# Fetching an expert's three weight matrices as three transfers instead of six halves, in a single-core encoder layer with a mixture of experts

## The chip, the cores and the metric

One core of one Trainium2 chip runs the whole kernel. The metric is the device time of one execution in microseconds (us); lower is better. All arithmetic inputs are float32.

## The reference, cut to what matters

The layer works on 1536 tokens (512 and 1024) with a model width of 1024. After a retention and an attention part it ends in a hierarchical mixture of 32 gated experts, of which each token uses two:

```python
pg = softmax(xt @ w_rg); g_sel = argmax(pg)                     # one of 4 groups
le_sel = (xt @ w_re)[group g_sel]; top_p, top_i = top_k(softmax(le_sel), 2)
gate = p_sel * top_p / sum(top_p)
# the 3072 (token, expert) pairs are sorted by expert and padded to blocks of 128 rows
def expert_block(xb, e):
    return (silu(xb @ w_g[e]) * (xb @ w_u[e])) @ w_d[e]         # 1024->512, 1024->512, 512->1024
y[token] += gate * expert_block(...)                            # two experts add to each token
x = rmsnorm(x + y) * g_final
```

Each expert has a gate, an up and a down matrix of 2 MB, so a block of 128 rows needs 6 MB of weights.

## The kernel before, in words

`build` (line 2010) runs five phases one after the other: `phase_project`, `phase_retention`, `phase_latent`, `phase_mix` (output projection, router, and a table in DRAM that lists for every expert the rows that chose it), and `phase_experts` (line 1671). The change touches the last two.

**Buffers.** `raw` (line 2032) holds one expert's three matrices as they come from DRAM: 128 partitions by 3 matrices by 4096 float32. On a partition a matrix is one run of 16 KB, in DRAM as well (line 2034). There is one `raw`, not two. Each matrix is treated as two halves of 2048 columns; `raw_span` (line 1666) gives the columns of half j, and j runs from 0 to 5: gate 0 and 1, up 2 and 3, down 4 and 5. `w_hi` and `w_lo` (line 1687) hold the same weights split into a rounded part and a rest; a product is made of three matmul passes over them (`three_passes`, line 108).

**Order of a block.** `each_block` (line 1726) runs two blocks written out and then a loop over pairs, 32 blocks in this execution. For block n:

- SyncE, `load` (line 1740): for each half j it waits until VectorE has split that half for block n-1 (`s_wlo[j]`) and then issues the half's transfer of 1 MB (lines 1745 to 1747). The first block's six halves are issued at the end of `phase_mix` (line 1401), before the experts begin.
- ScalarE, `step` (line 1888): `split(j, n)` for j 0 to 3 waits for the half to land (`s_raw[j]`, line 1870) and for the matmuls of the block before that used it, and writes `w_hi`. Then it takes its half of the previous block's result (`take_y`), the silu, `split` 4 and 5, the rounded part of the transposed hidden rows, and `rows_hi(n + 1)`.
- VectorE, `step` (line 1942): after each `w_hi` half it writes `w_lo` (line 1923). The order is halves 0 to 3, `take_y` of the previous block (line 1936), half 4, the product of the silu with the up result (line 1953), the rest of the hidden rows (line 1955), half 5, `rows_lo(n + 1)`.
- TensorE, `step` (line 1828): gate and up matmuls (`e_pg`, `e_pu`), then it waits for the gathered rows of block n+1 (`s_xg`, line 1841) and transposes the first half of them (`e_px`, line 1821), transposes the hidden rows (`e_ph`, line 1846), transposes the other half, and does the down matmuls (`e_py`).
- GpSimd, `step` (line 1786), with a DMA queue of its own: it copies the row numbers and shares of block n, then calls `gather(n + 2, ...)` (line 1766): a load of 128 table rows of 8 bytes (`e_who`, line 1768), a wait for it, an indirect load of 128 activation rows of 4 KB (`e_xg`, line 1772) and one of 128 shares of 4 bytes (`e_part`, line 1775). Then it waits for both halves of the result of block n and issues an indirect store that adds 128 rows of 4 KB into `x_mid` (line 1808).

All transfers, SyncE's (queue q1) and GpSimd's (queue q0), run on the same 16 DMA engines. The lines that set the order of the weight loads are these:

```python
for j in range(6):
    sp.wait_ge(s_wlo[j], n)
    sp.dma_start(raw[:, j // 2, span(j)], w_exp[j // 2][e][:, span(j)]).then_inc(s_raw[j], 16)
```

Of the kernel before, what the change touches and what calls it, by code (L numbers as in the profile page):

```python
# [1305 lines left out]
def phase_mix(nc, mixT, x_all, w_out, w_fold, g_ffn, w_rg, w_re, ident_d, route_d, blocks_d, x_mid, h_rows, table,  # L1306
              gates, blocks, n_pairs, s_tick, s_tock, raw, s_raw0, w_exp, shares):
    with ExitStack() as ctx:
# [60 lines left out]
        @block.sync  # L1369
        def _(sp):  # L1370
            sp.dma_start(ident[:], ident_d).then_inc(s_const, 16)
            sp.dma_start(route[:], route_d).then_inc(s_const, 16)
            sp.dma_start(g_row[:], g_ffn.partition_broadcast(P)).then_inc(s_const, 16)
            sp.dma_start(w_r[:, :, 0:NG], w_rg.rearrange("(p k) e -> p k e", k=KD)).then_inc(s_const, 16)
            sp.dma_start(w_r[:, :, NG:], w_re.rearrange("(p k) e -> p k e", k=KD)).then_inc(s_const, 16)
            sp.dma_start(blocks[:].rearrange("p a n -> p (a n)"), blocks_d).then_inc(s_const, 16)
            sp.dma_start(mx[:, 0, :], mixT[0]).then_inc(s_in[0], 16)
            sp.dma_start(xr[:, 0, :], x_all[0]).then_inc(s_xr[0], 16)
            w_v = w_out.rearrange("(k p) n -> p k n", p=P)
            for k in range(KD):  # L1380
                if k >= 3:
                    sp.wait_ge(s_wlo, k - 2)
                sp.dma_start(stage[:, k % 3, :],
                             w_v[:, k, :] if k < KD // 2 else w_fold[k - KD // 2]).then_inc(s_raw[k % 3], 16)

            def tile(r, half, last):
                t = 2 * r + half
                if not last:
                    behind = not (isinstance(r, int) and r == 0 and half == 0)
                    if behind:  # L1390
                        sp.wait_ge(s_mlo, t)
                        sp.wait_ge(s_const, 96)
                    sp.dma_start(mx[:, 1 - half, :], mixT[t + 1]).then_inc(s_in[1 - half], 16)
                    if behind:
                        sp.wait_ge(s_x2, t)
                        sp.wait_ge(s_const, 96)
                    sp.dma_start(xr[:, 1 - half, :], x_all[t + 1]).then_inc(s_xr[1 - half], 16)

            pairs(sp, TILES, tile)

            for j in range(6):
                sp.dma_start(raw[:, j // 2, raw_span(j)], w_exp[j // 2][0][:, raw_span(j)]).then_inc(s_raw0[j], 16)

        @block.gpsimd
        def _(pool):
# [265 lines left out]
def phase_experts(nc, w_exp, ident_d, h_rows, table, shares, blocks, n_pairs, s_tick, raw, s_raw, x_mid, g_final,  # L1671
# [4 lines left out]
    with ExitStack() as ctx:  # L1676
# [57 lines left out]
        @block.sync  # L1734
        def _(sp):
            sp.dma_start(ident[:], ident_d).then_inc(s_const, 16)
            sp.dma_start(g_row[:], g_final.partition_broadcast(P)).then_inc(s_const, 16)

            def load(r, half):
                n = 2 * r + half  # L1740
                if isinstance(r, int) and n == 0:
                    return
                e = n if isinstance(r, int) else sp.value_load(blocks[0:1, 0, bass.ds(n, 1)], min_val=0,
                                                               max_val=NE - 1)
                for j in range(6):
                    sp.wait_ge(s_wlo[j], n)
                    sp.dma_start(raw[:, j // 2, span(j)], w_exp[j // 2][e][:, span(j)]).then_inc(s_raw[j], 16)

            each_block(sp, load)

            pairs_done = pair_count(sp)
            for half in range(2):
                sp.wait_ge(s_store[half], 16 * pairs_done)
            for j in range(6):
                sp.dma_start(raw[:, j // 2, span(j)].rearrange("p (t n) -> p t n", t=2),
                             x_mid[2 * j:2 * j + 2].rearrange("t p n -> p t n")).then_inc(s_xmid[j], 16)
            for t in range(TILES):
                sp.wait_ge(s_out, t + 1)
                sp.dma_start(out[t], x_sum[t]).then_inc(s_kept, 16)
            sp.wait_ge(s_kept, 16 * TILES)  # L1760
# [106 lines left out]
        @block.scalar  # L1867
        def _(act):
            def split(j, n):
                act.wait_ge(s_raw[j], 16 * (n + 1))  # L1870
                free_after(act, j, n)
                nc.scalar.copy(w_hi[:, j // 2, span(j)], raw[:, j // 2, span(j)]).then_inc(s_whi[j], 1)  # L1872

            def rows_hi(n):
                for b in range(2):
                    act.wait_ge(s_xt, 2 * n + b + 1)
                    nc.scalar.copy(xT_hi[:, b * 512:(b + 1) * 512], px[:, b * 512:(b + 1) * 512]).then_inc(s_xhi, 1)

            def take_y(n, half):

                act.wait_ge(s_y, n + 1)
                act.wait_ge(s_code, n + 3)
                nc.scalar.activation(y_sb[half][:, 0:512], py[:, 0:512], ACT.Copy,
                                     scale=gate[half][:, 0:1]).then_inc(s_ya, 1)

            rows_hi(0)

            def step(r, half):
                n = 2 * r + half
                split(0, n)  # L1890
                split(1, n)
                split(2, n)
                split(3, n)
                if not (isinstance(r, int) and n == 0):
                    take_y(n - 1, 1 - half)
                act.wait_ge(s_gate, n + 1)
                nc.scalar.activation(act_g[:], pg[:], ACT.Silu).then_inc(s_silu, 1)
                split(4, n)
                split(5, n)
                act.wait_ge(s_ht, n + 1)  # L1900
                nc.scalar.copy(hT_hi[:], ph[:]).then_inc(s_hhi, 1)  # L1901
                rows_hi(n + 1)

            each_block(act, step)
            last = act.value_load(n_pairs[0:1, 1:2], min_val=0, max_val=(NE + MORE + 1) // 2)
            take_y(2 * last + 1, 1)

            act.wait_ge(s_eps, 1)

            for t in range(TILES):  # L1910
                act.wait_ge(s_xmid[t // 2], 16)
                act.wait_ge(s_rstd, t)
                one = slice(t, t + 1)
                nc.scalar.activation(junk, x_sum[t], ACT.Square, accum_out=ssq[:, one]).then_inc(s_sq, 1)  # L1914
                act.wait_ge(s_sq, t + 1)
                nc.scalar.activation(root[:, one], ssq[:, one], ACT.Sqrt, bias=eps[:],
                                     scale=1.0 / D).then_inc(s_root, 1)
# [92 lines left out]
def build(nc, d, out):  # L2010

    def scratch(name, shape, dt=F32):
        return nc.dram_tensor("s_" + name, shape, dt, kind="Internal").ap()

    mid = scratch("mid", (TILES, P, M_W))
    mixT = scratch("mixT", (TILES, P, D))
    w_fold = scratch("w_fold", (HM, P, D))
    x_mid = scratch("x_mid", (TILES + 1, P, D))
    h_rows = scratch("h_rows", (ROWS, D))
    shares = scratch("shares", (2 * ROWS, 1))  # L2020
    table = scratch("table", (NE * ROWS, 2), I32)

    with ExitStack() as ctx:
        s_tick, s_tock = (ctx.enter_context(nc.semaphore(n)) for n in ("tick", "tock"))
        phase_project(nc, d["x"], d["w_in"], d["g_mix"], d["g_q"], d["g_kv"], d["rope"], d["ident"], mid)
        phase_retention(nc, mid, d["log_decay"], d["gn_g"], d["dist"], d["index"], d["ident"], mixT)
        phase_latent(nc, mid, d["w_cat"], d["w_out"], d["rope"], d["ident"], mixT, w_fold)
        gates = ctx.enter_context(nc.sbuf_tensor("gates", [P, TILES, 2], F32))
        blocks = ctx.enter_context(nc.sbuf_tensor("blocks", [1, 2, NBLK], I32))
        n_pairs = ctx.enter_context(nc.sbuf_tensor("n_pairs", [1, 2], I32))  # L2030

        raw = ctx.enter_context(nc.sbuf_tensor("raw", [P, 3, 4096], F32))
        s_raw = [ctx.enter_context(nc.semaphore(f"raw{j}")) for j in range(6)]
        w_exp = [d[n].rearrange("e (p k) n -> e p (k n)", p=P) for n in ("w_gate", "w_up", "w_down")]
        phase_mix(nc, mixT, d["x"], d["w_out"], w_fold, d["g_ffn"], d["w_rg"], d["w_re"], d["ident"], d["route"],
                  d["blocks"], x_mid, h_rows.rearrange("(t p) n -> t p n", p=P), table, gates, blocks, n_pairs,
                  s_tick, s_tock, raw, s_raw, w_exp, shares)
        phase_experts(nc, w_exp, d["ident"], h_rows, table, shares, blocks, n_pairs, s_tick, raw, s_raw, x_mid,
                      d["g_final"], out)
# [20 lines left out]
```

## Time and profile before

| What | Value |
|---|---|
| Runs | 1805.31, 1809.92, 1807.42 us; median 1807.42 |
| The profiled execution's own time | 1802.13 us |
| Its span (first to last instruction) | 1800.6 us |
| TensorE matmul busy | 1494.7 us (83%) |
| VectorE busy | 1078.9 us (60%) |
| ScalarE busy | 835.3 us (46%) |
| GpSimd busy | 358.4 us (20%) |
| Read from DRAM / written | 288.61 MB / 63.87 MB |
| Loads into `raw` of gate, up, down | 64 each of 1024 KB; median from issue to landing 6.6, 9.6, 8.2 us |

The expert phase lasts from about 1094 us to the end. Times in rows are microseconds from the start of the span. A line of the timeline has start, duration, engine, source line, operation, output and inputs, and in brackets the idle time before it with what ended it; "x4" means four instructions merged, of which the first start and the whole duration are given.

### The profile page before, as it was taken

The page shows a single profiled execution, that of the slowest core. Times are in us where ns is not written, and L with a number is a line of the kernel's source. Part 1 is how long each engine was busy: PE and PEld are TensorE (multiplying, and loading weights), DVE is VectorE, ACT ScalarE, POOL GpSimd, SP SyncE. Part 2 cuts the span into 40 slices and gives each one's busy share as a digit, 9 for nine tenths or more (in the row PEclk, how much of TensorE's full clock was granted, in tenths as well). Part 3 has the DMA queues.
Part 4 walks back from the last instruction along what each step waited for, and adds up shares of the span by engine and source line. Part 5 has one row for each costly group of instructions (what it writes and reads, how often), then busy time and mean ns, then how long its engine had stood idle before and what let it go on. Part 6 is the DMA issues. An engine that isn't in the chain of part 4 may idle for free. (4 is left out here: it accounts for less than half of the span.)

```text
span 1800.6 us, 21880 instructions
## 1 busy us (share of the span) xinstructions
PE 1494.7 (83%) x7330; PEld 1224.4 (68%) x7330; DVE 1078.9 (60%) x1689; ACT 835.3 (46%) x1139; POOL 358.4 (20%) x327
## 2 busy tenths in 40 slices
PE   6799999954674779996699963999999999999990
PEld 5688888843673657885488852777777777777770
DVE  5322323224774656764345544888788887888784
ACT  5323232321564455543322213776667666766664
POOL 0000000000462000000011213233433433343330
PEclk9899999976675889999699976999999999999995
DMA  7121221224353110001633454999999999999977
GB/s 260 49 97 61 83 83 61 84 81 151 106 175 119 59 65 24 13 12 38 216 116 133 135 215 138 319 359 362 355 355 360 357 361 353 357 361 358 360 234 291
DMA packets 83585, 347.35 MB, mean 193 GB/s; under 512 B 14514, under 2 KB 25922, under 8 KB 57282
## 3 DMA queue, kind: packets, MB, share of 16 engines
q1 hardware_dynamic: 66434, 300.37, 45.6%
q0 software_dynamic: 17104, 46.38, 9.2%
q8 instruction: 26, 0.43, 0.1%
q14 instruction: 21, 0.17, 0.0%
HBM read 288.61 MB, written 63.87 MB: 196 GB/s over the span
## 5 line engine op out<-in xcount | busy, mean ns | idle before, releaser
L1923 DVE TENSOR_TENSOR e_w_lo<-raw,e_w_hi 128x2048 fp32r<-128x2048 f32 x192 | 430.8, 2285 | 40.9 <-ACT e_w_hi L1872 40.9
L1872 ACT CAST e_w_hi<-raw 128x2048 fp32r<-128x2048 f32 x192 | 353.8, 1921 | 0.0
L110 PE MATMUL a_pG<-a_w_hi,a_xT_hi 128*128 128x512 f32 (+1 forms) x480 | 189.8, 395 | 8.7 <-DVE a_w_lo L353 6.1
L112 PE MATMUL a_pG<-a_w_hi,a_xT_lo 128*128 128x512 f32 (+1 forms) x480 | 186.5, 388 | 0.0
L111 PE MATMUL a_pG<-a_w_lo,a_xT_hi 128*128 128x512 f32 (+1 forms) x480 | 186.1, 388 | 0.0
L1772 POOL DMA_INDIRECT e_xg<-s_h_rows,e_who x34 | 84.2, 2477 | 261.3 <-DMA e_who<-s_table 137.9
L110 PE MATMUL e_py<-e_w_hi,e_hT_hi 128*128 128x512 f32 x256 | 104.3, 408 | 30.4 <-DVE e_hT_lo L1955 30.4
L110 PEld LDWEIGHTS a_pG<-a_w_hi,a_xT_hi 128*128 128x128 f32 x480 | 91.2, 190 | 25.9 <-issue 5.5
L110 PE MATMUL e_pg<-e_w_hi,e_xT_hi 128*128 128x512 f32 x256 | 104.3, 408 | 4.9 <-DVE e_w_lo L1923 4.9
L110 PE MATMUL d_po<-d_w_hi,d_mT_hi 128*128 128x512 f32 x192 | 81.7, 426 | 26.0 <-DVE d_w_lo L1552 26.0
L112 PEld LDWEIGHTS a_pG<-a_w_hi,a_xT_lo 128*128 128x128 f32 x480 | 91.1, 190 | 17.2
L111 PEld LDWEIGHTS a_pG<-a_w_lo,a_xT_hi 128*128 128x128 f32 x480 | 91.3, 190 | 15.7
L111 PE MATMUL e_pg<-e_w_lo,e_xT_hi 128*128 128x512 f32 x256 | 101.8, 398 | 0.0
L112 PE MATMUL e_pg<-e_w_hi,e_xT_lo 128*128 128x512 f32 x256 | 101.7, 397 | 0.0
L112 PE MATMUL e_py<-e_w_hi,e_hT_lo 128*128 128x512 f32 x256 | 101.1, 395 | 0.0
L112 PE MATMUL e_pu<-e_w_hi,e_xT_lo 128*128 128x512 f32 x256 | 101.0, 395 | 0.0
L110 PE MATMUL e_pu<-e_w_hi,e_xT_hi 128*128 128x512 f32 x256 | 101.0, 395 | 0.0
L111 PE MATMUL e_pu<-e_w_lo,e_xT_hi 128*128 128x512 f32 x256 | 101.0, 394 | 0.0
L111 PE MATMUL e_py<-e_w_lo,e_hT_hi 128*128 128x512 f32 x256 | 101.0, 394 | 0.0
L1280 DVE TENSOR_TENSOR c_pT_lo<-c_pt,c_pT_hi 128x512 fp32r<-128x512 f32 x80 | 52.1, 684 | 46.8 <-ACT c_pT_hi L1131 46.8
L112 PE MATMUL d_po<-d_w_hi,d_mT_lo 128*128 128x512 f32 x192 | 79.9, 416 | 0.0
L111 PE MATMUL d_po<-d_w_lo,d_mT_hi 128*128 128x512 f32 x192 | 79.9, 416 | 0.0
(314 smaller groups left out, 3092.2 us busy)
## 6 DMA issues: line engine op xcount, KB each, us to landing
raw<-in_w_gate SPq DMA_DIRECT2D x64, 1024.0 KB, 6.6
raw<-in_w_up SPq DMA_DIRECT2D x64, 1024.0 KB, 9.6
raw<-in_w_down SPq DMA_DIRECT2D x64, 1024.0 KB, 8.2
s_mid<-a_rec SPq DMA_DIRECT2D x12, 1536.0 KB
a_x_sb<-in_x SPq DMA_DIRECT2D x12, 512.0 KB, 6.4
b_kv<-s_mid SPq DMA_DIRECT2D x12, 512.0 KB, 4.1
b_qk<-s_mid SPq DMA_DIRECT2D x12, 512.0 KB, 4.1
b_vg<-s_mid SPq DMA_DIRECT2D x12, 512.0 KB, 5.5
```

The lines of the kernel that those rows point to most:

```text
L110: pe.matmul(out, st_hi, mv_hi, start=first, stop=False)
L111: pe.matmul(out, st_hi, mv_lo, start=False, stop=False)
L112: return pe.matmul(out, st_lo, mv_hi, start=False, stop=last)
L1280: nc.vector.tensor_tensor(pT3_lo[:, 4 * i:4 * i + 4, j * P:(j + 1) * P], pt[:, c * 512:(c + 1) * 512].rearrange("p (k i) -> p k i", k=4), ...
L1772: pool.indirect_dma_start(out=xg[half][:], out_offset=None, in_=h_rows, in_offset=bass.IndirectOffsetOnAxis(ap=who[half][:, 0:1], axis=0), ...
L1872: nc.scalar.copy(w_hi[:, j // 2, span(j)], raw[:, j // 2, span(j)]).then_inc(s_whi[j], 1)
L1923: nc.vector.tensor_tensor(w_lo[:, j // 2, span(j)], raw[:, j // 2, span(j)], w_hi[:, j // 2, span(j)].bitcast(F32), ALU.subtract).then_inc ...
```

## The change

The loads of `raw` go from two per matrix to one per matrix, in both places where they are issued. The single load waits for both halves of the matrix to have been split. The semaphores of landing go from six to three, and ScalarE's split of either half waits for the whole matrix. The splits themselves stay in halves, and the order of instructions on ScalarE, VectorE, TensorE and GpSimd stays as it is.

```diff
-            for j in range(6):
-                sp.dma_start(raw[:, j // 2, raw_span(j)], w_exp[j // 2][0][:, raw_span(j)]).then_inc(s_raw0[j], 16)
+            for m in range(3):
+                sp.dma_start(raw[:, m, :], w_exp[m][0]).then_inc(s_raw0[m], 16)
...
-                for j in range(6):
-                    sp.wait_ge(s_wlo[j], n)
-                    sp.dma_start(raw[:, j // 2, span(j)], w_exp[j // 2][e][:, span(j)]).then_inc(s_raw[j], 16)
+                for m in range(3):
+                    sp.wait_ge(s_wlo[2 * m], n)
+                    sp.wait_ge(s_wlo[2 * m + 1], n)
+                    sp.dma_start(raw[:, m, :], w_exp[m][e]).then_inc(s_raw[m], 16)
...
             def split(j, n):
-                act.wait_ge(s_raw[j], 16 * (n + 1))
+                act.wait_ge(s_raw[j // 2], 16 * (n + 1))
...
-        s_raw = [ctx.enter_context(nc.semaphore(f"raw{j}")) for j in range(6)]
+        s_raw = [ctx.enter_context(nc.semaphore(f"raw{j}")) for j in range(3)]
```

## Rows read from the trace of the kernel before

**Rows 1.** Windows, one stretch: us, busy by engine, PE clock, DMA share, GB/s.

```profile
1400.00:1500.00 100.00, 94.50 (x419) 74.23 (x418) 82.25 (x56) 67.84 (x55) 36.97 (x31) 1.00 1.01 359
```

**Rows 2.** Waits, 1200 to 1700 us: who waited for whom, us, times, longest.

```profile
DVE e_w_lo L1923 <- ACT e_w_hi L1872: 28.9, 25, 1.2
...
PEld e_px L1821 <- DMA e_part<-s_shares,e_who: 16.8, 22, 1.3
...
PE e_px L1821 <- DMA e_part<-s_shares,e_who: 6.9, 15, 0.8
```

**Rows 3.** Chain that ended last, one round of two blocks: start, us, what.

```profile
1446.80 0.71 PE e_px L1821 x4
...
1466.83 7.88 DMA e_who<-s_table
...
1475.69 2.69 POOL e_xg L1772
...
1478.69 8.19 DMA e_part<-s_shares,e_who
1486.92 0.71 PE e_px L1821 x4
```

**Rows 4.** Timeline of GpSimd, the adding store of one block.

```profile
1463.39 1.63 POOL L1808 DMA_INDIRECT s_x_mid<-e_y_sb,e_code  x1 [2.91 <-issue]
```

**Rows 5.** Timeline of TensorE, transposes of hidden rows in four blocks.

```profile
1124.81 0.75 PE L1846 MATMUL e_ph<-e_ident,e_h_sb 128*128 128x128 f32 x4 [0.41 <-DVE e_h_sb L1953]
1749.27 0.75 PE L1846 MATMUL e_ph<-e_ident,e_h_sb 128*128 128x128 f32 x4 [0.41 <-DVE e_h_sb L1953]
...
1205.70 0.64 PE L1846 MATMUL e_ph<-e_ident,e_h_sb 128*128 128x128 f32 x4
1225.67 0.75 PE L1846 MATMUL e_ph<-e_ident,e_h_sb 128*128 128x128 f32 x4 [0.41 <-DVE e_h_sb L1953]
```

**Rows 6.** Timeline of SyncE's queue: the two issues of each matrix.

```profile
1459.63 2.54 SPq L1747 DMA_DIRECT2D raw<-in_w_up  x2
1465.93 6.29 SPq L1747 DMA_DIRECT2D raw<-in_w_down  x2
1475.43 2.54 SPq L1747 DMA_DIRECT2D raw<-in_w_gate  x2
```

**Rows 7.** DMA issues: up half issued at 1461.83, down half at 1471.89; us to landing.

```profile
raw<-in_w_up SPq DMA_DIRECT2D x1, 1024.0 KB, 11.1
...
raw<-in_w_down SPq DMA_DIRECT2D x1, 1024.0 KB, 6.4
```

**Rows 8.** Timeline of ScalarE: splits 0 to 3, then splits 4 and 5.

```profile
1469.79 7.36 ACT L1872 CAST e_w_hi<-raw 128x2048 fp32r<-128x2048 f32 x4
...
1481.75 3.70 ACT L1872 CAST e_w_hi<-raw 128x2048 fp32r<-128x2048 f32 x2
```

**Rows 9.** DMA issues: down half issued at 1123.13 onto a nearly empty queue.

```profile
raw<-in_w_down SPq DMA_DIRECT2D x1, 1024.0 KB, 5.9
```

**Rows 10.** DMA queues, 1460 to 1480.1 us (one block): packets, MB, share.

```profile
q1 hardware_dynamic: 866, 6.29, 82.0%
q0 software_dynamic: 352, 0.93, 19.2%
```

**Rows 11.** DMA queues, 1046.5 to 1049.5 us, weights with little beside them.

```profile
q1 hardware_dynamic: 173, 1.21, 96.4%
```

**Rows 12.** DMA queues, 380 to 385 us, one store of 12 KB per partition.

```profile
q1 hardware_dynamic: 144, 1.57, 75.0%
```

**Rows 13.** DMA queues, 1461.5 to 1465.5 us, a gather beside weights.

```profile
q1 hardware_dynamic: 164, 1.20, 72.8%
q0 software_dynamic: 165, 0.40, 27.2%
```

**Rows 14.** DMA queues, 1467.6 to 1472 us, an adding store beside weights.

```profile
q0 software_dynamic: 107, 0.44, 52.0%
q1 hardware_dynamic: 117, 0.84, 48.3%
```

## The prediction

> **What bounds the kernel now.** The change acts on the expert phase alone, so I read that stage, not the whole span. The windows view comes first: in 1400 to 1500 us TensorE is busy 94.5 of 100 us at a granted clock of 1.00 (the 2.4 GHz level), VectorE 82, and the DMA engines are busy all the time at 359 GB/s [rows 1]. So three things are near their limit at once, and only waits tell which one ends last. In the waits view from 1200 to 1700 us (25 blocks) VectorE's splits wait only for ScalarE's, 28.9 us in all, and no row says that a split on ScalarE waits for `raw`: **no weight load is late**. TensorE waits for one transfer, the gathered rows: 16.8 us at the weight load and 6.9 us at the matmul, two views of partly the same waits [rows 2]. The chain of waits confirms it. It runs in rounds of two blocks: `e_px` at 1446.80, VectorE's splits, GpSimd's store at 1463.39 [rows 4], the 8-byte table rows (`e_who`, 7.88 us), the gather (2.69 us), the shares (`e_part`, 8.19 us), and `e_px` two blocks on at 1486.92 [rows 3]. That is 40.12 us for two blocks, of which 16.1 us is the landing time of two tiny transfers that share the DMA engines with the weights. From the first to the last transpose of hidden rows lie 1749.27 - 1124.81 = 624.5 us for 31 intervals, 20.14 us a block; a fast interval is 1225.67 - 1205.70 = 19.97 us [rows 5]. Since hardly any interval of the trace is shorter, I take 19.97 us as what TensorE and its partners need with no late gather. The chain can therefore grow at full price, but shrink by only 31 x 0.17 = 5 us.
>
> **Fewer issues.** SyncE issues three transfers fewer per block. Its time is free: it waits for VectorE between issues, 2.5 us for two up or gate issues and 6.3 us for the two of down [rows 6]. Gain 0. In `phase_mix` three issues drop out after the last tile's loads; the experts start some 60 us later, so 0 there.
>
> **When the loads start and land.** The last half of each matrix is issued at the same moment as before; only the first half is held back, by about 2.2 us for gate and up and by 6.0 us for down (1465.93 to 1471.89) [rows 6].
> - Up: its second half, issued at 1461.83, lands 11.1 us later, at 1472.9 [rows 7]. The queue is served in order with the same bytes ahead, so the whole matrix lands at 1472.9 as well. Before, split 3 needed it at 1469.79 + 3 x 1.84 = 1475.3; now split 2 does, at 1473.5 [rows 8]. The spare falls from 2.4 to 0.6 us. Cost 0, with the thinnest cover of all; if the landing slips by 1 us, ScalarE, then VectorE's splits and the store behind them slip by 0.4 us per block.
> - Down: up's bytes occupy the queue until about 1472.9, and the first half of down could not move before that anyway. Issued whole at 1471.89 onto a queue about to empty, it pays a start. 1 MB on a nearly empty queue lands in 5.9 us [rows 9], and in a stretch full of weights q1 moves 1.21 MB in 0.964 x 3 us, 418 GB/s [rows 11], which is 2.5 us for a 1 MB half. So down lands by 1471.9 + 5.9 + 2.5 = 1480.3. Split 4 reads it at 1481.75 [rows 8]. Spare 1.4 us, cost 0.
> - Gate: whole at 1477.6, by the same sum at 1486.0, needed at 1469.79 + 20.1 = 1489.9. Cost 0.
>
> **Larger packets beside the gather: the term that decides.** A block shows 866 packets of q1 for 6.29 MB, one per partition and half (768 of 8 KB) plus small ones [rows 10]. A store with rows of 12 KB shows 144 packets for 1.57 MB, again one per row [rows 12], so a row of 16 KB should be one packet of 16 KB. Beside each other the two queues take turns packet by packet: 164 to 165 in the gather's stretch [rows 13], 117 to 107 in the store's [rows 14]. A weight packet of 8 KB holds one of 16 engines for 8192 B x 16 / 418 GB/s = 0.31 us; one of 16 KB for 0.63 us.
> - Gather and shares: 0.40 MB in rows of 4 KB is 97 rows, 6 per engine [rows 13]. Each waits for one weight packet, now 0.31 us longer: 6 x 0.31 = **1.9 us later** per round of two blocks, if gate's 16 KB packets are there all the time. The bounds are 0 (it falls into a gap) and 8 x 0.31 = 2.5 us.
> - The adding store, behind which `e_who` waits in the same queue: by the same sum up to 8 x 0.31 = 2.5 us later. But down's first half, which ran beside it since 1465.93, is now issued only at 1471.89, near the store's end. The engines have the same bytes to move up to that moment, less down's, so the larger packets are offset. I take 0; bounds -1 and +2.5 us.
>
> **The sum.** Fully beside gate the chain grows by 1.9 us per two blocks, 0.95 us a block. But gate's first half is no longer in the queue when the gather is posted (1475.69 to 1478.4) [rows 3]; whole, it starts at 1477.6, about when down's bytes end. So part of the gather goes ahead of it, the more so the longer a block gets, since VectorE's part of the round starts anew at each `e_px` while the gather comes earlier against it. Between 0 and 0.95 I take the middle, 0.48 us for each of 30 blocks: **+14 us**. The profiled execution lies at 1802.1 us (span 1800.6), 5 us under the median of the runs shown, 1807.4; it would come to 1816, and the runs to **1821 us**.
>
> **Two rules against the rows.** The trace has 8 KB and 12 KB rows as single packets. The Trainium skill (DMA: Bandwidth & Descriptors, Queues, rings and completion order) says that an engine takes turns between queue rows and drains a whole packet before switching. By that rule this sum stands; the trace agrees in its near equal counts [rows 13, 14], but no run yet shows 16 KB rows. The same page (Rules for kernel authors, and the fit in its anatomy of a DMA) speaks the other way: transfers of 1 MB and more, each with about 2.0 us fixed. Three fewer per block would then be an estimated 6 us a block, some 190 us in all, if transfers followed one another alone.
>
> **Rivals.**
> - *Nothing measurable, -5 to +5 us.* The gather finds the gap between down and gate, and every load keeps its spare. For it: spares are positive by the rows, and the chain's excess over 19.97 us is small. Against: 0.6 us under up. Some 1809 us.
> - *Faster: fewer transfer starts.* q1 is busy 82% of 20.1 us, 16.5 us, for 6.29 MB that take 15.0 us at 418 GB/s [rows 10, 11]; 1.5 us a block is lost, perhaps at starts. Half of it back is 0.7 us of queue, and `e_part` lands earlier. It decides once the round falls below two TensorE blocks, and there it stops: 31 x 0.17 = 5 us, 1802 us. Against: the starts are hidden while other bytes flow.
> - *Much slower: both stretches at full price.* Store and gather each meet 16 KB packets all the way, 2.5 + 1.9 = 4.4 us per round, 2.2 us a block, 66 us: 1873 us. For it: equal turns in both stretches. Against: down is not there beside the store. A late up matrix lands here too: 1 us over its spare in each block is 31 us or less.
> - *The change does not do what it says:* a row of 16 KB is cut into 8 KB packets. Then only the issue times move, and it is the first rival.
>
> **How the numbers follow.** Chances: the forecast, 5 to 30 us slower, 0.45; nothing measurable 0.29; faster 0.09; much slower 0.17. About 0.3% (5.4 us) is what a measurement of this kernel can tell from no change; the runs shown spread by 0.25%. So faster 0.09, same 0.29, slower 0.62. The range reaches down into no change and the edge of faster, 1802, and up to two thirds of the full price, 1858; about 0.06 is left below and 0.12 above.
>
> **What the profile would show.** Right: q1 has 384 packets of 16 KB a block and small ones; `e_part` lands in 9 to 10 us instead of 8.2; waits of `e_px` for it grow by 10 us or more; intervals of 20.5 us and more; no row "`e_w_hi` waits for DMA `raw`". Wrong if packets stay at 8 KB, if ScalarE waits for `raw` (then the landing of up was the step that failed), if `e_who` lands in 10 us (then the store), or if intervals shrink towards 20.0 us.

## The result, and the profile after

The changed kernel takes **1855.05 us** (median of 4 runs, 1841.02 to 1860.94) against 1808.13 us before (4 runs, 1805.31 to 1809.92): ratio 1.025, 95% interval 1.019 to 1.031. It is slower, as forecast, and inside the range, but by 47 us where 14 were forecast. The profiled execution took 1860.94 us (span 1859.4), 58.8 us more than the one of before.

**Where the time is.** First and last transposes of hidden rows, TensorE's timeline; then those of three blocks with the gathered rows' transposes beside them (start, us, what, in brackets the idle time before):

```profile
1130.57 0.75 PE L1847 MATMUL e_ph<-e_ident,e_h_sb 128*128 128x128 f32 x4 [0.41 <-DVE e_h_sb L1954]
1807.67 0.75 PE L1847 MATMUL e_ph<-e_ident,e_h_sb 128*128 128x128 f32 x4 [0.41 <-DVE e_h_sb L1954]
...
1477.65 0.75 PE L1847 MATMUL e_ph<-e_ident,e_h_sb 128*128 128x128 f32 x4 [0.41 <-DVE e_h_sb L1954]
...
1500.96 1.12 PE L1822 MATMUL e_px<-e_ident,e_xg 128*128 128x128 f32 x4 [4.08 <-DMA e_part<-s_shares,e_who]
1501.87 1.06 PE L1847 MATMUL e_ph<-e_ident,e_h_sb 128*128 128x128 f32 x4
...
1524.71 0.75 PE L1847 MATMUL e_ph<-e_ident,e_h_sb 128*128 128x128 f32 x4 [0.41 <-DVE e_h_sb L1954]
...
1544.84 0.75 PE L1847 MATMUL e_ph<-e_ident,e_h_sb 128*128 128x128 f32 x4 [0.41 <-DVE e_h_sb L1954]
```

31 intervals in 677.1 us are 21.84 us each, 1.70 more than before [rows 5]: 52.6 of the 58.8 us. Nearly all of the rest, 5.7 us, is there already when SyncE issues the very first load of `raw` (1039.22 us, before 1033.53), so ahead of anything that the change touches. In the kernels below the first transpose moves between 1122.5 and 1133.9 us, in those with the first loads of before as well; I leave it out. The intervals are of three kinds. Eleven are as before, 20.10 us on average. Ten hold a wait of TensorE for the shares, 2.6 to 4.2 us: together 36.4 us over 20.09. The ten that follow those are 17.8 us over it, and seven of them (22.0 to 23.1 us) make 16.9 of that. What those seven hold shows in the windows, cut at the transposes above:

```profile
1457.50:1477.60 20.10, 18.76 (x84) 14.99 (x84) 16.53 (x11) 13.57 (x11) 7.68 (x6) 1.00 0.92 330
1477.60:1501.90 24.30, 19.22 (x85) 15.34 (x86) 16.54 (x11) 13.57 (x11) 8.06 (x6) 0.95 1.00 347
1501.90:1524.70 22.80, 21.86 (x85) 17.48 (x83) 16.53 (x11) 13.66 (x11) 6.99 (x6) 0.82 0.83 298
1524.70:1545.00 20.30, 18.93 (x85) 15.15 (x86) 16.53 (x11) 13.58 (x11) 6.62 (x6) 1.00 0.88 310
...
1496.90:1501.00 4.10, 0.04 (x1) 0.05 (x1) 0.69 (x1) 0.00 (x0) 0.59 (x1) 0.84 0.98 319
1501.00:1505.00 4.00, 3.45 (x14) 2.95 (x15) 1.42 (x2) 2.04 (x4) 0.00 (x0) 0.50 0.69 164
1505.00:1509.00 4.00, 4.00 (x11) 3.14 (x10) 4.00 (x4) 4.00 (x3) 2.69 (x2) 0.50 0.37 82
...
1305.00:1308.50 3.50, 2.82 (x12) 2.42 (x12) 0.21 (x1) 0.83 (x2) 0.00 (x0) 0.52 0.97 254
```

The block after the wait has the same 85 matmuls, but they keep TensorE busy for 21.9 instead of 18.8 us, at a granted clock of 0.82. TensorE stood idle for 4.1 us until 1501, and from there to 1509 it has 0.50, the 1.2 GHz level; before, and in the blocks that neither hold nor follow a wait, it has 1.00. The last row is from one of the other three of those ten: behind a wait of 3.6 us the clock is low for about 3 us alone, and the next block takes 20.4 us.

**Who is waited for.** The waits of 1200 to 1700 us (us, times, longest), the same stretch as [rows 2]:

```profile
DVE e_w_lo L1924 <- ACT e_w_hi L1873: 36.5, 23, 3.6
PEld e_px L1822 <- DMA e_part<-s_shares,e_who: 28.3, 7, 4.5
PE e_px L1822 <- DMA e_part<-s_shares,e_who: 25.3, 7, 4.1
...
ACT e_w_hi L1873 <- DMA raw<-in_w_up: 0.6, 1, 0.6
```

Before, TensorE had 15 such waits of 0.8 us at most; now it has 7, the longest 4.1. ScalarE waits once, for 0.6 us, for a weight load. The chain of waits, with its links on TensorE inside the block left out:

```profile
1410.72 7.55 DMA e_who<-s_table
...
1419.25 3.06 POOL e_xg L1773
...
1422.61 11.97 DMA e_part<-s_shares,e_who
1434.63 1.07 PE e_px L1822 x4
```

Against [rows 3] the table rows are no later (7.55, before 7.88 us), the gather's issue is about the same (3.06, before 2.69), and the shares alone have grown: **11.97, before 8.19 us**. In the whole chain of before they land after 8.2 to 8.9 us, in the ten late blocks of the changed kernel after 10.6 to 12.2. GpSimd's timeline shows why this comes in one block of three:

```profile
1485.54 2.92 POOL L1773 DMA_INDIRECT e_xg<-s_h_rows,e_who  x1 [8.06 <-issue]
1488.76 1.86 POOL L1776 DMA_INDIRECT e_part<-s_shares,e_who  x1 [0.30 <-issue]
...
1506.01 1.38 POOL L1773 DMA_INDIRECT e_xg<-s_h_rows,e_who  x1 [8.44 <-DMA e_who<-s_table]
1507.69 3.05 POOL L1776 DMA_INDIRECT e_part<-s_shares,e_who  x1 [0.30 <-issue]
...
1529.67 1.04 POOL L1773 DMA_INDIRECT e_xg<-s_h_rows,e_who  x1 [8.13 <-issue]
```

and SyncE's, the loads beside them:

```profile
1487.76 0.34 SPq L1748 DMA_DIRECT2D raw<-in_w_gate  x1
1492.09 0.33 SPq L1748 DMA_DIRECT2D raw<-in_w_up  x1
1506.61 0.33 SPq L1748 DMA_DIRECT2D raw<-in_w_down  x1
1512.29 0.33 SPq L1748 DMA_DIRECT2D raw<-in_w_gate  x1
...
1534.82 0.34 SPq L1748 DMA_DIRECT2D raw<-in_w_gate  x1
```

The gather of 1485.54 and the shares of 1488.76 have gate, then up, right beside them, and the shares land at 1500.91. Once TensorE has stood still for 4 us, the next two gathers go out 6.3 and 5.2 us ahead of gate, and the shares issued at 1507.69 land after 7.8 us. Then the lead is used up and the next one is late. That holds all through the trace: the ten late gathers were issued 1.7 to 2.4 us ahead of gate, the others 2.5 to 6.3 us.

Where the late shares lose their time, DMA queues again, from 1491.8 to 1496 us and from 1496 to 1498.6:

```profile
q0 software_dynamic: 159, 0.38, 23.0%
...
q0 software_dynamic: 12, 0.02, 2.4%
```

The first row of this gather moves at 1491.87, 3.1 us after the issue of the shares (before 2.9 us, at 1481.63), so the start is no later. Most of its small transfers are through by 1496; the last few follow one by one until 1500.6, while the weights keep the engines busy. From the first row to the last share it takes 8.7 us, before 4.8.

**The packets.** DMA queues of the changed kernel, 1400 to 1500 us, then 1509 to 1512 us, where the weights have the engines nearly alone:

```profile
q1 hardware_dynamic: 2048, 29.89, 78.7%
...
q1 hardware_dynamic: 75, 1.23, 96.2%
```

In the short stretch 75 packets carry 1.23 MB, 16.4 KB each: a row of 16 KB is one packet, and takes 0.962 x 48 / 75 = 0.62 us (forecast 0.63).

### The profile page after: what moved, and what is told of

Read it like the earlier page. It is cut to its first block and busy times, and to the rows that moved or that the text cites. A ratio compares the mean times of both kernels' runs of the same rounds, so it can differ in the third digit from the quotient of the medians.

```text
span 1859.4 us, 21757 instructions
## 1 busy us (share of the span) xinstructions
PE 1519.6 (82%) x7330; PEld 1246.3 (67%) x7330; DVE 1080.9 (58%) x1689; ACT 836.4 (45%) x1139; POOL 346.8 (19%) x327
## 5 line engine op out<-in xcount | busy, mean ns | idle before, releaser
L110 PE MATMUL e_py<-e_w_hi,e_hT_hi 128*128 128x512 f32 x256 | 111.4, 435 | 26.6 <-DVE e_hT_lo L1956 26.6
L1773 POOL DMA_INDIRECT e_xg<-s_h_rows,e_who x34 | 64.5, 1897 | 252.5 <-DMA e_who<-s_table 135.7
L111 PE MATMUL e_py<-e_w_lo,e_hT_hi 128*128 128x512 f32 x256 | 107.0, 418 | 0.0
L112 PE MATMUL e_py<-e_w_hi,e_hT_lo 128*128 128x512 f32 x256 | 106.6, 416 | 0.0
L1822 PE MATMUL e_px<-e_ident,e_xg 128*128 128x128 f32 x264 | 49.6, 320 | 59.5 <-DMA e_part<-s_shares,e_who 59.5
L1809 POOL DMA_INDIRECT s_x_mid<-e_y_sb,e_code x32 | 53.1, 1659 | 191.9 <-issue 102.6
L1822 PEld LDWEIGHTS e_px<-e_ident,e_xg 128*128 128x128 f32 x264 | 41.8, 201 | 65.9 <-DMA e_part<-s_shares,e_who 40.9
```

What stands on the lines that cost most here:

```text
L110: pe.matmul(out, st_hi, mv_hi, start=first, stop=False)
L111: pe.matmul(out, st_hi, mv_lo, start=False, stop=False)
L112: return pe.matmul(out, st_lo, mv_hi, start=False, stop=last)
L1773: pool.indirect_dma_start(out=xg[half][:], out_offset=None, in_=h_rows, in_offset=bass.IndirectOffsetOnAxis(ap=who[half][:, 0:1], axis=0), ...
L1809: pool.indirect_dma_start(out=x_rows, out_offset=bass.IndirectOffsetOnAxis(ap=code[half][:, 0:1], axis=0), in_=y_sb[half][:], in_offset=No ...
L1822: ins = pe.transpose(px[:, k * P:(k + 1) * P], xg[half][:, k:D:KD], ident[:])
```

## The experiments

All ratios are against the kernel before, run in turn on the same chip (medians of 1804.98 to 1807.3 us there).

**1. The hold-back alone.** Six halves with rows of 8 KB as before, but both halves are issued together when the whole matrix is split.

```diff
-                for j in range(6):
-                    sp.wait_ge(s_wlo[j], n)
-                    sp.dma_start(raw[:, j // 2, span(j)], w_exp[j // 2][e][:, span(j)]).then_inc(s_raw[j], 16)
+                for m in range(3):
+                    sp.wait_ge(s_wlo[2 * m], n)
+                    sp.wait_ge(s_wlo[2 * m + 1], n)
+                    for j in (2 * m, 2 * m + 1):
+                        sp.dma_start(raw[:, m, span(j)], w_exp[m][e][:, span(j)]).then_inc(s_raw[j], 16)
```

> Six transfers with rows of 8 KB as before, but both halves of a matrix are issued together, when both have been split; so the issue times are those of the changed kernel and the packets those of the kernel before. Theory P (packets of 16 KB delay the gathered rows): time within 5 us of the kernel before, about 1808 us, mean interval of blocks 20.0 to 20.3 us, few waits of e_px over 1 us. Rival H (holding back the first halves costs the time, through gaps in the DMA engines' work and loads that meet the gather): about the changed kernel's time, 1845 to 1860 us, with waits of e_px of 3 to 4 us in one block of three.

Measured: 1805.04 us (10 runs, 1797.99 to 1810.21), ratio 0.9991 (0.9974 to 1.0007); interval 20.07 us. Its wait for the shares, 1200 to 1700 us:

```profile
PE e_px L1823 <- DMA e_part<-s_shares,e_who: 1.8, 7, 0.4
```

So the later issue costs nothing, and the loss comes from the form of the transfers.

**2. Packets cut with the descriptor's shape.** The same three transfers, each row written as two pieces of 8 KB; the pieces lie side by side.

```diff
-                    sp.dma_start(raw[:, m, :], w_exp[m][e]).then_inc(s_raw[m], 16)
+                    sp.dma_start(raw[:, m, :].rearrange("p (q n) -> p q n", q=2),
+                                 w_exp[m][e].rearrange("p (q n) -> p q n", q=2)).then_inc(s_raw[m], 16)
```

> The changed kernel with three transfers, but each row of 16 KB written as two pieces of 8 KB in one transfer. If the pieces are packets of their own (768 packets of q1 a block), theory P expects the time of the kernel before, within 5 us; rival H, and any cause that lies in the number of transfers, expects 1845 to 1860 us. If the pieces are joined again (384 packets), the run repeats the changed kernel and tells nothing.

Measured: 1856.23 us (1846.31 to 1856.88), ratio 1.0267 (1.0242 to 1.0293); interval 21.27 us. Queue q1 from 1400 to 1500 us:

```profile
q1 hardware_dynamic: 2049, 29.90, 77.7%
```

2049 packets where the changed kernel had 2048: neighbouring pieces were joined into rows of 16 KB again. The run says nothing on packets, but it repeats the changed kernel in five more runs, and its loss with it.

**3. Rows of 4 KB, the same way, in the kernel before.**

```diff
-                    sp.dma_start(raw[:, j // 2, span(j)], w_exp[j // 2][e][:, span(j)]).then_inc(s_raw[j], 16)
+                    sp.dma_start(raw[:, j // 2, span(j)].rearrange("p (q n) -> p q n", q=2),
+                                 w_exp[j // 2][e][:, span(j)].rearrange("p (q n) -> p q n", q=2)).then_inc(s_raw[j], 16)
```

> The kernel before with its six transfers, rows of 8 KB cut in two pieces of 4 KB. Theory P carried on downwards: a packet beside the gather holds an engine 0.16 us instead of 0.31, the round of two blocks shortens by up to 0.9 us and the small waits of e_px (0.2 to 0.8 us) go; TensorE's 19.97 us a block are the floor, so 3 to 5 us faster than before, 1803 us. Rival (smaller packets cost the engines bandwidth, and the weights come late): slower than before by 5 us or more, with waits of ScalarE for raw.

Measured: 1806.28 us, ratio 0.9996 (0.9981 to 1.0012). Joined as well (4285 packets of q1 for 31.17 MB from 1400 to 1500 us, before 4311 for 31.42), so it is the kernel before, and what packets under 8 KB would do stays open.

**4. Three transfers, packets of 8 KB.** The two halves of a matrix lie 32 bytes apart in SBUF, so a row can't be one packet. Everything else is the changed kernel.

```diff
-        raw = ctx.enter_context(nc.sbuf_tensor("raw", [P, 3, 4096], F32))
+        raw = ctx.enter_context(nc.sbuf_tensor("raw", [P, 3, 2, 2056], F32))
...
-                    sp.dma_start(raw[:, m, :], w_exp[m][e]).then_inc(s_raw[m], 16)
+                    sp.dma_start(raw[:, m, :, 0:2048],
+                                 w_exp[m][e].rearrange("p (q n) -> p q n", q=2)).then_inc(s_raw[m], 16)
```

> The changed kernel with its three transfers, but in SBUF the two halves of a matrix lie 32 bytes apart, so that a row is two runs of 8 KB and cannot be joined to one packet: 768 packets of q1 a block, three transfers. Theory P (the packet's size is the cause): the kernel before within 5 us, about 1807 us, mean interval 20.1 us. Rival T (it is the transfer of 2 MB as one, whatever its packets): 1845 to 1860 us, intervals of 24 us in one block of three.

Measured: 1807.99 us (10 runs), ratio 1.0 (0.9987 to 1.0014); interval 20.08 us. Its queue q1 from 1400 to 1500 us:

```profile
q1 hardware_dynamic: 4051, 31.22, 77.8%
```

and its waits, 1200 to 1700 us:

```profile
ACT e_w_hi L1875 <- DMA raw<-in_w_up: 35.5, 23, 2.2
...
PEld e_px L1824 <- DMA e_part<-s_shares,e_who: 0.4, 1, 0.4
```

Twice the packets, the same number of transfers, and the loss is gone with the wait for the shares. **The size of the packets is the cause**, not the fewer transfers; nor is it the pattern with two pieces, which experiment 2 has too, with the whole loss. Up now lands after 13.2 us (median of 1400 to 1500 us) instead of 11.2, and ScalarE waits for it in nearly every block, 1.5 us on average, without any cost in time.

**5. The same packets, the gather moved ahead.** The changed kernel, but GpSimd does a block's copies, look-up, the store of the block before, and then the gather, so that the table rows land while the store is prepared.

```diff
-                gather(n + 2, r + 1, half, ahead)
+                look_up(n + 2, r + 1, half, ahead)
+                if not (isinstance(r, int) and n == 0):
+                    store(n - 1, r - 1 + half, 1 - half)
+                fetch(n + 2, r + 1, half)
```

> The changed kernel with another order on GpSimd: row numbers copied and table rows looked up ahead of the store of the block before, then the store, then the gather. The store's landing still starts the next round (about 11 us, 2.3 us of copies, a look-up of 2 to 8 us, under 20 us together), and the gather is issued right behind the store, about 10 us earlier than now. If the late gather is the only way in which the change costs time: no wait of e_px over 1 us, intervals of 20.0 to 20.1 us, granted clock 1.00 all through, 1800 to 1808 us. If up's thin spare or bandwidth costs as well: ScalarE waits for raw and the time stays over 1812 us.

Measured: 1803.48 us (10 runs, 1796.16 to 1806.19), ratio 0.9982 (0.9966 to 0.9997); interval 20.09 us; TensorE never waits for the shares, and its clock is 1.00. One block on GpSimd:

```profile
1442.36 0.59 POOL L1768 DMA_DIRECT2D e_who<-s_table  x1 [0.75 <-POOL e_gate L1803]
1447.58 1.63 POOL L1819 DMA_INDIRECT s_x_mid<-e_y_sb,e_code  x1 [4.64 <-DVE e_y_sb L1949]
1449.52 1.48 POOL L1778 DMA_INDIRECT e_xg<-s_h_rows,e_who  x1 [0.31 <-issue]
```

TensorE's next transposes of gathered rows:

```profile
1470.83 0.60 PE L1834 MATMUL e_px<-e_ident,e_xg 128*128 128x128 f32 x4
```

The gather's issue now lies 21.3 us ahead of them, where it was 1486.92 - 1475.69 = 11.2 us [rows 3]. With packets of 16 KB all through, the loss is gone: the late gather was its only way to the end. The kernel is a hair faster than the one before.

**6. The same order with the six halves of before.** The edit of 5 in the kernel before.

> The kernel before with the same new order on GpSimd. The waits of e_px for e_part (about 8 us in all) go; TensorE and VectorE set the interval, 19.97 to 20.08 us against 20.14 us: 2 to 5 us faster than before. Rival: the store, now followed closely by the gather, or the look-up beside other transfers makes a new wait; then as before or slower.

Measured: 1804.85 us (12 runs), ratio 0.9986 (0.9973 to 0.9999). The intervals overlap with those of 5: given this order, three transfers or six are the same.

**7. The gather ahead of the store.** In the changed kernel, the adding store is moved behind the next gather, without the early look-up of 5 (its new place is shown, the old one is empty).

```diff
                 gather(n + 2, r + 1, half, ahead)
+                if not (isinstance(r, int) and n == 0):
+                    store(n - 1, r - 1 + half, 1 - half)
```

> The changed kernel (16 KB packets, held back), with GpSimd's adding store of a block moved behind the gather for the block after next, so that table rows and gathered rows no longer wait for VectorE's half of the result and for the store. If the late gather is the only way in which the change costs time, no wait of e_px is left, intervals are 20.0 to 20.1 us, the granted clock stays 1.00, and the time is at or a little under the kernel before, 1800 to 1808 us. Rival (up lands late: its spare was 0.6 us, or the engines lack bandwidth): ScalarE waits for raw and the time stays 10 us or more above the kernel before.

Measured: 1882.42 us, ratio 1.0412 (1.038 to 1.0444), worse than the changed kernel. GpSimd's timeline:

```profile
1465.00 1.04 POOL L1773 DMA_INDIRECT e_xg<-s_h_rows,e_who  x1 [2.43 <-DMA e_who<-s_table]
...
1468.75 2.52 POOL L1813 DMA_INDIRECT s_x_mid<-e_y_sb,e_code  x1 [0.30 <-issue]
1482.97 0.18 POOL L1797 COPY e_code<-e_who 128x1 int32<-128x1 int32 x1 [11.70 <-DMA s_x_mid<-e_y_sb,e_code]
1483.10 0.17 POOL L1798 COPY e_gate<-e_part 128x1 f32<-128x1 f32 x1
1484.03 0.60 POOL L1769 DMA_DIRECT2D e_who<-s_table  x1 [0.75 <-POOL e_gate L1798]
1487.08 1.05 POOL L1773 DMA_INDIRECT e_xg<-s_h_rows,e_who  x1 [2.44 <-issue]
```

The copies overwrite what the store reads, so they wait until it has landed, 14.2 us after its issue, and the gather is behind them. A ring over two blocks became one over a single block: 1487.08 - 1465.00 = 22.1 us. What I expected failed for this reason, and the run does not test the theory; 5 does.

**8 and 9. One matrix, or two.** Only gate whole (16 KB rows), and only up and down whole; the rest in halves, everything held back as in 1. For gate:

```diff
+                    if m in (0,):
+                        sp.dma_start(raw[:, m, :], w_exp[m][e]).then_inc(s_raw[2 * m], 16)
+                        continue
+                    for j in (2 * m, 2 * m + 1):
+                        sp.dma_start(raw[:, m, span(j)], w_exp[m][e][:, span(j)]).then_inc(s_raw[j], 16)
```

> Only gate comes as one transfer with rows of 16 KB; up and down come in two halves with rows of 8 KB, all issued when the matrix has been split, so the issue times are those of the changed kernel. In the changed kernel's trace the late gathers are served while gate (issued 3 us before the shares, landing 8.5 us later) is in the queue. If gate's packets are what delays them: most of the changed kernel's loss, 1830 to 1860 us, waits of e_px of 2 to 4 us. If it takes 16 KB packets everywhere, or those of up or down: 1805 to 1815 us.

> The counterpart: up and down as one transfer each with rows of 16 KB, gate in two halves of 8 KB rows. If gate's packets are the cause: 1805 to 1815 us, waits of e_px under 1.5 us. If up's packets, which follow gate while the last gathered rows are served, weigh as much: 1820 us or more.

Measured: gate 1822.02 us, ratio 1.0076 (1.0046 to 1.0105), interval 20.53 us; up and down 1809.13 us (10 runs, 1800.17 to 1822.15), ratio 1.0015 (0.998 to 1.0049), interval 20.38 us. The wait for the shares, 1200 to 1700 us, with gate whole:

```profile
PE e_px L1830 <- DMA e_part<-s_shares,e_who: 14.2, 9, 2.0
```

and with up and down whole:

```profile
PE e_px L1830 <- DMA e_part<-s_shares,e_who: 8.5, 12, 2.7
```

Gate, which runs beside the gather, costs some 14 us and up and down 3, which can't be told from none; all three cost 47. They don't add up, and gate alone lies between the two ranges that I expected. With gate alone the longest wait is 2.0 us and the clock stays at 1.00 in each of the windows 1400 to 1700 us; with all three the waits reach 4.2 us and the clock falls behind each of them. With up and down whole the runs spread over 22 us, and the trace of one of them has two waits above 1 us, of 1.9 and 2.7. Behind both the clock falls and the next block takes 22.4 us; behind the one of 1.9 us:

```profile
1205.50:1212.30 6.80, 6.25 (x19) 4.88 (x19) 5.41 (x5) 6.03 (x6) 0.07 (x1) 0.50 0.86 200
```

**10 and 11. Rows of 16 KB in six transfers.** The changed kernel with each matrix in two transfers of 64 partitions with whole rows: first the lower and upper 64 partitions, then the even and odd ones.

```diff
-                    sp.dma_start(raw[:, m, :], w_exp[m][e]).then_inc(s_raw[m], 16)
+                    for a in (0, 64):
+                        sp.dma_start(raw[a:a + 64, m, :], w_exp[m][e][a:a + 64]).then_inc(s_raw[m], 16)
...
-                    sp.dma_start(raw[:, m, :], w_exp[m][e]).then_inc(s_raw[m], 16)
+                    for a in (0, 1):
+                        sp.dma_start(raw[a::2, m, :], w_exp[m][e][a::2]).then_inc(s_raw[m], 16)
```

> Six transfers of 1 MB again, issued two by two when a matrix has been split, but cut by partitions: 64 rows of 16 KB each, so 384 packets of 16 KB a block in six transfers. Theory P: like the changed kernel, 1840 to 1860 us, waits of e_px of 3 to 4 us. Rival T: the kernel before within 5 us.

> Six transfers of 64 rows of 16 KB again, but one takes the even and one the odd partitions instead of the lower and the upper 64. In the run cut at partition 64 a packet of 16 KB took 1.2 to 1.3 us instead of 0.61, and the kernel 2177 us. If that came from writing to one half of the partitions only: here packets take 0.61 us again and, by theory P, the time is that of the changed kernel, 1840 to 1860 us; with the rival that the number of transfers matters, it is the kernel before's. If the slow packets come from transfers of 64 rows as such, it stays near 2177 us.

Measured: halves of the partitions 2177.18 us, ratio 1.2035 (1.2003 to 1.2066); alternate partitions 1830.46 us, ratio 1.013 (1.0083 to 1.0176). The lower and upper halves, the window of 1400 to 1500 us and queue q1 from 1464 to 1470 us:

```profile
1400.00:1500.00 100.00, 68.13 (x271) 54.24 (x270) 52.29 (x35) 44.30 (x35) 19.71 (x20) 0.80 1.01 224
```

```profile
q1 hardware_dynamic: 93, 1.26, 100.6%
```

Here the engines are busy all the time and move 224 GB/s. Of the 93 packets 77 are rows of 16 KB (1.26 MB), so each takes about 1.006 x 96 / 77 = 1.25 us, twice the 0.62 of the changed kernel. With alternate partitions they take 0.61 us again (median of the packets of 1200 to 1700 us). That matches what the Trainium skill (SBUF — State Buffer, Door 1: The DMA port swizzle) says: bit 6 of the partition number picks which of a cluster's two ports a write goes through, so the lower 64 partitions reach half of the ports, and even ones reach all.

The wait with alternate partitions, 1200 to 1700 us:

```profile
PE e_px L1824 <- DMA e_part<-s_shares,e_who: 23.6, 13, 4.1
```

Six transfers with 16 KB packets are slow as well, by the same wait. Its loss of 24 us is half of the changed kernel's and less than I expected; why not all of it stays open. Transfers of 1 MB from alternate partitions give another pattern in time, and no run separates that.

## Why the prediction was right or wrong

**The bound, right.** The wait for gathered rows ended last with no slack, so that the round could grow at full price and hardly shrink. The best order found (5) gains 3 us, where I allowed 5. The floor was read a little low: with no wait at all the interval is 20.09 us (5), and the intervals of 19.97 us in the trace of before stand behind blocks that a wait had made longer.

**Fewer issues and the hold-back, 0 forecast, right.** Experiment 1: ratio 0.9991, no difference. The landings of one block of the changed kernel were 8.5 us for gate (forecast 8.4), 11.3 for up (11.1) and 8.7 for down (8.4). The thin cover of up held but for one wait of 0.6 us. The price that I put on its loss was too high: I wrote 0.4 us per block for each 1 us of slip, and experiment 4 has waits of 1.5 us in nearly every block with an interval of 20.08 us.

**The store, 0 forecast, right.** The store lands after 10.8 us (median of 1200 to 1700 us; 12.0 at most), before 10.7 (11.2), and in the chain `e_who` behind it after 7.55 us, before 7.88. The bound of +2.5 us was not reached.

**Packets and turns, right.** Rows of 16 KB are single packets of 0.62 us; experiment 4 shows that their size, and 5 that the gather behind them, carries the whole loss. The first two rivals and the one with cut packets fall. Of the third, the direction was right, the place (both stretches at full price) was not.

**The gather's price, the step that failed.** I took "6 rows per engine", the mean of 97 rows of hidden vectors, by 0.31 us: 1.9 us, with 2.5 as the upper bound. Measured: the late shares land after 11.9 us (median of those in the chain) instead of 8.5, **3.4 us later**, and 3.8 to 4.0 in the two blocks shown (11.97 and 12.15 against 8.19). Two things were left out, both in view. [rows 13] has 165 packets of that queue, and I counted the 97 that its 0.40 MB make; the small rows of the shares take turns too. A block has 96 real rows on average (3072 pairs in 32 blocks; the padding's table rows point outside, and the bounds check of the indirect loads drops them), so with the shares there are 12 turns per engine and not 6: 12 x 0.31 = 3.7 us. And the wait ends with the slowest engine, not with the mean: the last shares follow the bulk of them by over 4 us. A full block has 16 turns, at most 5.0 us. Which engine lags, and why, the trace does not say.

**How often, right in kind, near by luck.** I took half of the full price because a longer block lets the gather pass ahead of gate. That feedback is there: one block in three is late, the next two are not. But the half was the middle between two bounds and not worked out. Ten waits cost 36.4 us over 31 intervals, 1.17 us a block; with 3.4 us in place of 1.9 my own step (half of a round's price, per two blocks) gives 0.85 us, 26 us in all. So the gather's delay was put at little more than half of its size, and the share of late blocks (10 of 31, where half of the rounds means a quarter) was nearly right.

**The clock, missing.** The sum held no term for TensorE's clock. Behind each of the ten waits the granted clock fell to 0.50. In seven cases (waits of 2.6 to 4.2 us) it stayed there for 7 to 10 us, and the next block took 2 to 3 us longer: 16.9 us in all, a third of the loss. In the other three the waits were as long (3.6 to 4.1 us), the fall lasted about 3 us, and the next block took 20.4 us. The length of the wait alone does not decide it: in experiment 2 a wait of 3.6 us had no fall behind it and a next block of 20.04 us, and with up and down whole one of 1.9 us had a fall. With gate alone whole (waits up to 2.0 us) the clock did not fall and the loss was 14 us. That the fall costs the 17 us is read from these rows; no run held the wait and removed the fall. What the ten blocks with waits (36.4 us) and the ten behind them (17.8 us) have over 20.09 us, less the 1.7 us that the intervals of before had over it, is the 52.6 us of the intervals.

**The range, kept by luck.** Two thirds of the full price of 66 us on top of 1807 are 1851 us; the 1858 that I gave as its upper end are over three quarters. The measured 1855 lies between the two, and one of the four runs (1860.94) above both. That the range reached so far was owed to a rival that did not occur, the store at full price, and not to the two terms that were short, the gather's price and the clock.

**The two rules.** The Trainium skill's turn-taking (DMA: Bandwidth & Descriptors, Queues, rings and completion order) stands: a packet twice as long holds its engine 0.62 instead of 0.31 us, and the small packets of the other queue came late by it. The gain that I estimated from the fixed 2.0 us per transfer of the same page of the Trainium skill (Anatomy of one DMA) did not appear: experiments 4 and 1 differ in three transfers or six (and the gap of 32 bytes), and take 1808 and 1805 us; 5 and 6 differ in the same way (and in packets of 16 or 8 KB), and take 1803 and 1805.

## What to carry to other kernels

Where small transfers share the DMA engines with a bulk load and somebody waits for them, the length of the bulk rows is a latency: count every packet of the small transfer that an engine serves, those of a few bytes too, by the price of one bulk packet, and take the fullest engine. Then look at what the waiting engine loses besides the wait: behind some 4 us of idle TensorE the next block often took 2 to 3 us more, at the lower clock. The cure was not in the loads but in posting the small transfers sooner, or in keeping the bulk rows at 8 KB.

## What the runs showed of the hardware that was not expected

- Neighbouring pieces of a row are joined into one packet (2049 packets with the pieces, 2048 without); a gap of 32 bytes in SBUF keeps them apart (4051).
- Writes to one half of the partitions take twice as long per packet (1.25 instead of 0.62 us) and bring 224 GB/s; with every second partition it is 0.61 us and 347 GB/s (1400 to 1500 us in both).
- A wait for weights on ScalarE of 1.5 us in almost every block cost nothing, while a wait of TensorE often cost more than its own length.
- The granted clock fell to 0.50 behind a TensorE wait of 1.9 us in one run and stayed at 1.00 behind one of 3.6 us in another.
